# Two tiles' pair sums and their selection, head by head behind the scores instead of at the beginning of the experts' first product

## What is computed

```python
q = (hb @ w_q).reshape(n, 8, 2, 128)                      # 8 heads, two halves each
s = jnp.einsum('nhid,hikd->nhik', q, sub_keys)            # 128 scores a head and half
s_top, i_top = lax.top_k(s, 16)
cand = s_top[:, :, 0, :, None] + s_top[:, :, 1, None, :]  # sums of pairs, 16 x 16
cand_idx = i_top[:, :, 0, :, None] * 128 + i_top[:, :, 1, None, :]
best, pos = lax.top_k(cand.reshape(n, 8, 256), 16)
idx = jnp.take_along_axis(cand_idx.reshape(n, 8, -1), pos, axis=-1)
w = jax.nn.softmax(best, axis=-1)
act = jax.nn.gelu(jnp.einsum('nhkd,nd->nhk', jnp.take(u_tab, idx, axis=0), hb))
out = jnp.einsum('nhk,nhkd->nd', w * act, jnp.take(v_tab, idx, axis=0))
```

## Time and profile before

| | us |
|---|---|
| median of 3 runs | 3179.07 (3177.73 to 3181.28) |
| profiled execution | 3177.63 |
| its span on the core | 3175.8 |
| TensorE busy | 3065.7 (97%) |
| VectorE busy | 2172.2 (68%) |
| ScalarE busy | 1153.6 (36%) |

### The profile page before, as it was taken

One profiled execution on the slowest core, in us unless ns is written; L12 is line 12 of the kernel. 1 busy time (PEld: TensorE's weight loads), 2 busy tenths in 40 slices (PEclk: granted clock), 3 DMA queues, 4 the chain that ended last, 5 costly groups with the idle time before them and its releaser, 6 DMA issues.

```text
span 3175.8 us, 43036 instructions
## 1 busy us (share of the span) xinstructions
PE 3065.7 (97%) x17723; PEld 2805.4 (88%) x17723; DVE 2172.2 (68%) x3782; ACT 1153.6 (36%) x1569; POOL 409.2 (13%) x264
## 2 busy tenths in 40 slices
PE   7999998999999999999999999999999999999998
PEld 7888887878879888988877879999999989999998
DVE  6536875755743433577663468898897859889997
ACT  2224233222233341555553232344444533333332
POOL 0000000000000000000000000010111226656552
PEclk9888999999999998999999999999999999999999
DMA  6223113222232124212224333547768899999996
GB/s 233 96 106 146 41 42 119 76 87 102 76 125 84 67 107 144 80 58 78 79 100 160 125 113 117 199 162 245 259 227 288 297 311 401 402 402 403 401 400 236
DMA packets 215714, 571.10 MB, mean 180 GB/s; under 512 B 14288, under 2 KB 129488, under 8 KB 180064
## 3 DMA queue, kind: packets, MB, share of 16 engines
q1 hardware_dynamic: 176496, 426.14, 37.3%
q0 software_dynamic: 36864, 134.23, 11.2%
q10 hardware_dynamic: 2160, 7.99, 0.7%
HBM read 495.95 MB, written 72.35 MB: 179 GB/s over the span
## 4 chain that ended last, share of the span: by engine, by line
PE 74%; DVE 14%; DMA 8%; ACT 3%; issue 1%; SPq 0%; DVEq 0%; ACTq 0%
PE bank L579 66%; DMA wv<-weight_spill 6%; DVE wl L534 3%; PE bank L1242 3%; DVE acc L149 2%; PE bank L643 2%; DMA gelu_spill<-gst 1%; PE bank L2513 1%; PE bank L591 1%; PE bank L650 1%; DVE Ah L3048 1%; DVE ub L3272 1%; PE bank L2522 1%; DVE pl L3215 1%; DVE gv L3204 1%
## 5 line engine op out<-in xcount | busy, mean ns | idle before, releaser
L579 PE MATMUL bank<-hh,wh 128*128 128x512 f32 (+2 forms) x2512 | 918.7, 366 | 17.2 <-DVE wl L534 7.1
L579 PE MATMUL bank<-hl,wh 128*128 128x512 f32 (+2 forms) x2512 | 895.0, 356 | 0.0
L579 PE MATMUL bank<-hh,wl 128*128 128x512 f32 (+2 forms) x2512 | 889.9, 354 | 0.0
L534 DVE TENSOR_TENSOR wl<-ring,wh 128x2048 fp32r<-128x2048 f32 (+2 forms) x249 | 554.3, 2226 | 288.0 <-ACT wh L527 287.4
L527 ACT ACTIVATE wh<-ring 128x2048 fp32r<-128x2048 f32 (+2 forms) x249 | 463.8, 1862 | 784.7 <-PE bank L579 763.0
L579 PEld LDWEIGHTS bank<-hh,wh 128*128 128x128 f32 x2512 | 480.7, 191 | 72.5 <-issue 17.8
L579 PEld LDWEIGHTS bank<-hl,wh 128*128 128x128 f32 x2512 | 480.7, 191 | 50.0 <-issue 6.0
L579 PEld LDWEIGHTS bank<-hh,wl 128*128 128x128 f32 x2512 | 481.1, 192 | 46.3
L579 PE MATMUL bank<-ph,wh 128*128 128x384 f32 x1024 | 348.1, 340 | 17.2 <-DVE pl L3215 10.5
L3258 POOL DMA_INDIRECT ub<-in_urow,gsel x112 | 180.0, 1607 | 1385.9 <-DVE gsel L2975 875.9
L579 PE MATMUL bank<-ph,wl 128*128 128x384 f32 x1024 | 346.3, 338 | 0.0
(11 more groups left out here) (522 smaller groups left out, 4461.2 us busy)
## 6 DMA issues: line engine op xcount, KB each, us to landing
ring<-in_v SPq DMA_DIRECT2D x68, 1024.0 KB
ring<-in_u SPq DMA_DIRECT2D x64, 1024.0 KB
ring<-in_ada SPq DMA_DIRECT2D x24, 1024.0 KB
gelu_spill<-gst SPq DMA_DIRECT2D x128, 192.0 KB
weight_spill<-stage SPq DMA_DIRECT2D x24, 1024.0 KB, 12.1
gv<-gelu_spill SPq DMA_DIRECT2D x64, 384.0 KB
wv<-weight_spill SPq DMA_DIRECT2D x64, 384.0 KB
ring<-in_wup SPq DMA_DIRECT2D x22, 1024.0 KB
```

The source lines that it names most:

```text
L534: v.then_inc(v.e.tensor_tensor(wl[q % 2][:, 0:n], ring[k % 4][:, 0:n], wh[q % 2][:, 0:n].bitcast(F32), S_), s("parts"))
L579: ins = p.e.matmul(out, l, r, start=start and i == 0, stop=stop and i == len(pairs) - 1, skip_group_check=not check)
```

## The change

For token tiles 0 and 1 the sums of pairs and the selection over them move from `top(0)` and `top(1)` into the loop of scores. There, whenever the selections of a head's second half are made (n odd), VectorE makes that head's two sums and the selection over 112 values, for both token tiles: `early_pairs_ve`. The results have places of their own (`bests`, `pixs`, in `Bh`), and the sums (`early`) lie in `ub`. `top(0)` and `top(1)` have 9 steps in place of 17, and `CHOOSE` goes from 1.14 to 1.07, so that the 271 steps (287 before) take 253 of the 256 calls (252 before). A wait for the landing of the second spill of x (`xsp`) is added before the first turn; that spill was issued at 1837.9 us.

```diff
+    bests = [by_h8(Bh[0][:, 2 * j, :]) for j in range(2)] + [by_h8(spare[:, 5, :])] * 2
+    pixs = [by_h8(Bh[0][:, 2 * j + 1, :].bitcast(U32)) for j in range(2)] + [by_h8(spare[:, 6, :].bitcast(U32))] * 2
+    early = [ub[j][:, 0:896].rearrange("p (h c) -> p h c", h=8) for j in range(2)]
...
+    def early_pairs_ve(v, j, h):
+        v.settle()
+        pairs = tops[j][:, 2 * h:2 * h + 2, :]
+        for a0, a1, nb_, at in ((0, 4, 16, 0), (4, 16, 4, 64)):
+            shape = [128, a1 - a0, nb_]
+            v.then_inc(v.e.tensor_tensor(early[j][:, h, at:at + (a1 - a0) * nb_].rearrange("p (a b) -> p a b", b=nb_),
+                                         pairs[:, 0, a0:a1].unsqueeze(2).to_broadcast(shape),
+                                         pairs[:, 1, 0:nb_].unsqueeze(1).to_broadcast(shape), A_), s("ve"))
+        top16(v, bests[j][:, h, :], pixs[j][:, h, :], early[j][:, h, :], sr[:, 0:112])
+
+    def early_turn_ve(v, n):
+        early_ve(v, n)
+        if n == 1:
+            v.wait_ge(s("xsp"), 32)
+        if n % 2:
+            for j in range(2):
+                early_pairs_ve(v, j, n // 2)
...
     def top_idle(j):
-        for _ in range((11 if j >= EARLY else 0) + 1 + 8 + 1 + 6 + 1):
+        for _ in range((11 + 8 if j >= EARLY else 0) + 1 + 1 + 6 + 1):
...
-    CHOOSE = 1.14
+    CHOOSE = 1.07
```

More of the change, by code:

```diff
@@ L73 @@
     [("g2_ex", 1), ("g3_ex", 1), ("sga", 16)],
-    [("ve", 1261), ("fin", 8)],
+    [("ve", 1289), ("fin", 8)],
     [("ada_sum", 22), ("go_rc", 4), ("r1", 8), ("fc", 44), ("qk_v", 8), ("glo", 2), ("G", 5), ("vm", 4), ("om", 8), ("up", 8), ("raw0", 2), ("dt_v", 2), ("ctm", 8), ("gm", 8), ("r2", 8), ("pq", 16), ("seld", 8),
@@ L471, in _build @@
     paf = [spare[:, 3 + c, 0:64].bitcast(B16) for c in range(2)]
-    best, pix = by_h8(spare[:, 5, :]), by_h8(spare[:, 6, :].bitcast(U32))
+    bests = [by_h8(Bh[0][:, 2 * j, :]) for j in range(2)] + [by_h8(spare[:, 5, :])] * 2
+    pixs = [by_h8(Bh[0][:, 2 * j + 1, :].bitcast(U32)) for j in range(2)] + [by_h8(spare[:, 6, :].bitcast(U32))] * 2
+    early = [ub[j][:, 0:896].rearrange("p (h c) -> p h c", h=8) for j in range(2)]
     hT = hhu[:, :, 16:16 + GT]
@@ L2884, in score_ve @@
             if n >= 3:
-                early_ve(v, n - 3)
+                early_turn_ve(v, n - 3)
         for n in range(13, 16):
-            early_ve(v, n)
+            early_turn_ve(v, n)
         end_ve(v)
@@ L2900, in top_sc @@
         w3 = sel[:, 2, :].rearrange("p (h k) -> p h k", h=8)
-        for _ in range((11 if j >= EARLY else 0) + 1 + 8 + 1 + 6):
+        for _ in range((11 + 8 if j >= EARLY else 0) + 1 + 1 + 6):
             yield
@@ L2908, in top_ve @@
         tt = v.e.tensor_tensor
-        top, tix = tops[j], tixs[j]
+        top, tix, best, pix = tops[j], tixs[j], bests[j], pixs[j]
         if j >= EARLY:
@@ L2921, in top_ve @@
             v.wait_ge(s("hT_mm"), 2)
[L2922 to L2928, removed]
+        if j >= EARLY:
+            pairs = top[:, :, :].rearrange("p (h c) k -> p h c k", c=2)
+            for a0, a1, nb_, at in ((0, 4, 16, 0), (4, 16, 4, 64)):
+                shape = [128, 8, a1 - a0, nb_]
+                v.then_inc(tt(cand[:, :, at:at + (a1 - a0) * nb_].rearrange("p h (a b) -> p h a b", b=nb_),
+                              pairs[:, :, 0, a0:a1].unsqueeze(3).to_broadcast(shape),
+                              pairs[:, :, 1, 0:nb_].unsqueeze(2).to_broadcast(shape), A_), s("ve"))
+            v.settle()
         keys = flat(top[:, 0:8, :]).bitcast(B16)[:, 0:256].rearrange("p (c a h) -> p c a h", c=2, a=16)
@@ L2933, in top_ve @@
         yield
-        for h in range(8):
-            top16(v, best[:, h, :], pix[:, h, :], cand[:, h, :], sr[:, 0:112])
-            yield
+        if j >= EARLY:
+            for h in range(8):
+                top16(v, best[:, h, :], pix[:, h, :], cand[:, h, :], sr[:, 0:112])
+                yield
         v.settle()
```

## The result

The changed kernel takes 3183.6 us (median of 12 runs, 3179.6 to 3190.1), the kernel before in the same rounds 3177.7 (12 runs, 3174.9 to 3181.3): ratio 1.0017, 95% interval 1.0010 to 1.0025. It is slower, as forecast, but by 5.4 us (3.2 to 7.9) and not by 15; that is less than the 6.4 us which the prediction said a measurement can tell from no change.

A forecast was written before the change was run, and what follows sets the result against it. TensorE, occupied for 97% of the span, was taken as the bound, so only its stalls and low clock count. Terms 15.2 + 2 - 4.9 - 6.7 + 9 = +14.6 us gave 3192.2 (profiled) or 3193.6 (median), range 3179 to 3205.

The forecast's parts named there:

- the handover: From first to second expert product: a later weight spill and `ph0` behind one more gelu cost +9 us (+4 to +13).
- nothing behind it absorbs a delay: Second product: bound by TensorE, so any delay that reaches it arrives in full at the end.
- the price of a turn: Loop of scores: one turn of sums and selections for both tiles takes VectorE 3.9 us (3.65 to 4.15).
- the backlog: Behind the loop of scores: VectorE reaches the third expert `wl` 16.4 us later, so TensorE loses +15.2 us (13.2 to 17.2).
- the waits for `pqT`: End of the loop of scores: the last two score products hold TensorE some 10 us, within the +15.2.
- the eight pairs: Front of the experts' first product: time lost to VectorE over eight pairs of expert tiles goes, -4.9 us (-2 at least).
- the interleaved stretches: Experts' first product: factor 1.07 shortens idle time and low clock, -6.7 us (-4, or -13.8 if both stay clear).
- The clock behind the front: After TensorE's waits in front: work at the lower clock behind the last wait costs +2 us (0 to 3.1).
- the front: Up to the end of the third pair of expert tiles: TensorE's waits and the clock, 15.2 + 2, cumulated +17.2 us.
- the clock rows: Experts' first product: a stall of 2 to 4 us costs about as much again in slow clock, 3.1 and 2 us.
- The slow first step: Start of the second product: its first step takes 8.46 us, and an idle clock adds up to 3 more.
- handover unmoved: Rival between the two expert products: the handover doesn't move, so +5.6 us in all, 3184.7; chance 0.17.

The follow-up runs named there:

- e2: Kernel before with only VectorE's work moved into the loop of scores, its old steps left empty and CHOOSE still 1.14: 3191.4 us, ratio 1.0044.
- e7: Kernel before with only the handover's order of the changed kernel: 3179.7 us, ratio 1.0008.
- e11: Changed kernel with 12 row gathers and their sums moved from the second product into the first's last interleaved stretch: 3182.0 us, ratio 1.0013.
- e13: Kernel before with 12 row gathers and their sums moved from the second product into the first's last interleaved stretch: 3166.6 us, ratio 0.9965.
- e4: Kernel before with 72 more matmuls in the second product's first step, making TensorE 12.5 us late: 3183.1 us, ratio 1.0019.
- e10: Kernel before with 41 of 182 row gathers beside the second product left out and 72 more matmuls in its first step: 3174.1 us, ratio 0.9990.
- e16: The same kernel as e10, measured once more against the kernel before: 3172.1 us, ratio 0.9983.
- e1: Changed kernel with CHOOSE 1.076 in place of 1.07, which puts the handover back in the old order: 3185.8 us, ratio 1.0030.

## Why the prediction was wrong, and what of it was right

The sum of +14.6 us failed at its last step. Up to the second product 10 us had come together and not 14.6, since the handover was put too high; and the sentence that nothing behind it absorbs a delay was wrong, for 3.4 of the 10 were left at the last tick (5.4 us in the time).

*Right: the price of a turn* (3.9 forecast, 3.9 measured), *the backlog* (third `wl` ready at 1987.1; measured 1987.5, from TensorE's matmul at 1990.76 less the 3.3), the waits for `pqT` of about 10 (9.3), the eight pairs (-4.9; -4.6 in e2), and, within its size, *the interleaved stretches* (-6.7; some -5). The clock behind the front was worth 0.3 us and not 2: the tick at the end of the third pair is +15.9 where the `wl` alone makes +15.6. The low clock fell between the waits (granted clock 0.78 and 0.54 in the two windows from 1950 to 1970, 1.00 from 1970 to 2000), where it only shortened the next wait. At the end of the first product the sum was off by 0.3 us, by luck in part: the front was 1.3 too high, the saving behind it 1.6. The prediction also read the clock rows wrongly: the 3.1 and 2 us that it calls the cost are time worked at the lower level, and not what was lost in it. By the starts of the matmuls, 0.32 us apart there and 0.175 at the full clock, the two places lost some 2.7 and 1.6 us, so the term moves by under half a us.

*Mis-sized: the handover.* The mechanism is as described, `ph` behind one gelu more and that behind a spill, but it moves the second step by 4 to 5.5 us and not by 9. The step that failed is the start of the second product. I left the gelu of tile 126 where the earlier trace rows have it and added 0 to 4 us for the spills; in e7 it came 2.2 us earlier: the spill that it waits for, that of tile 124, is issued at a relative 2600.3, ahead of the last weight spill, where before it was issued at 2602.07, behind it. The start came at 2612.5 where I had 2614.7 to 2618.5 (relative times, without the front's +5.9). The slow first step I had about right: 9.97 us in the changed kernel and 11.4 in e7, against 8.46 and up to 3 more. The term isn't a constant, either: with rows moved, end of the first product to end of the second step takes 36.2 us in e11 against 26.0 in e13, 10 more.

*Wrong: "Behind it, nothing absorbs a delay: the second product is bound by TensorE."* That sentence rested on the share of busy time of TensorE. The second product is bound by its transfers, by 0.2 us in a step, and by TensorE only while the buffers last. Of the 10 us that reached it, it gave 6.6 back in the profiled execution; in e4 some 6 of 12.5; in e10 and e16, with the transfers relieved, 1.6 and 3.6 of 12.5. The range held the time by luck: the forecast itself was +7 to +26, and its lower part was there for a rival (handover unmoved, 3184.7) with another reason.

What stays open: the front of e1 and e2 is 1.1 us later at the tick of 1980.36 than that of the changed kernel, though the turns are the same, and e1 is 2 us behind in the stretches; which of the places that the factor moves makes that was not tried. e2 lost 13.9 us in the second product and gave back little, although it started as late as the changed kernel did, and its median is 8 us above it where the traces differ by 4.8. e1 is like it: +9.0 at the end of the second step, +7.4 at the last tick, where the changed kernel goes from +10.0 to +3.4, e4 from +11.4 to +7.7 and e7 from +5.5 to +3.4. So what was given back differs with the place of the delay: little of one that comes from the front of the first product with the handover unmoved, more of one that hits TensorE at or behind the handover, when the loads are under way. A theory that knows only the time at which the second product starts doesn't explain this; how far the loads and the gathers have come by then may be what matters, and no run here measured it.

## What to carry to other kernels

Before writing that a delay arrives at the end, ask for the chain of each later stage by itself. An engine can be busy for 98% and still follow a load: set the bytes of one step over the rate against the engine's time for a step, and if the two differ by a few per cent, count the buffers. The DMA share alone doesn't decide it. And an edit that "costs nothing" may stand ahead of a stage that swallows it: repeat the comparison with that stage relieved, as e13 and e11 do, for that is nearer to the price you will pay when somebody mends it; and look at the terms too, since the edit that relieves the stage can change them.

## What I had not expected of the hardware

The rate of 402 GB/s in a stream of weights with indirect gathers beside it, within 1% in each 80 us of the 480; and that with gathers of half the partitions it was 261 GB/s in 2840 to 3000, so that asking for 122 x 256 KB less made the kernel 72 us slower.
